# A chunked scan's triangular inverses: two chunks under way at once, one PSUM bank each

## What is computed

```python
def step(state, inp):                      # RWKV-7, one token
    rt, wt, kt, vt, kkt, at = inp
    sa = jnp.einsum('bhij,bhj->bhi', state, -kkt)
    state = (state * wt[:, :, None, :] + sa[..., None] * (kkt * at)[:, :, None, :]
             + vt[..., None] * kt[:, :, None, :])
    return state, jnp.einsum('bhij,bhj->bhi', state, rt)
...
def step(state, inp):                      # HGRN2, one chunk
    scores = jnp.einsum('bhtd,bhsd,bhtsd->bhts', qc, kc, pair)
    out = (jnp.einsum('bhts,bhse->bhte', scores, vc)
           + jnp.einsum('bhtd,bhde->bhte', qc * jnp.exp(cum), state))
```

## Time and profile before

| | us |
|---|---|
| median of 3 runs | 3158.49 |
| lowest and highest run | 3154.6, 3160.9 |
| span of the profiled execution | 3156.2 |

### The profile page before, as it was taken

One profiled execution on the slowest core, in us unless ns is written; L12 is line 12 of the kernel. 1 busy time (PEld: TensorE's weight loads), 2 busy tenths in 40 slices (PEclk: granted clock), 3 DMA queues, 4 the chain that ended last, 5 costly groups with the idle time before them and its releaser, 6 DMA issues. The chain is left out here.

```text
span 3156.2 us, 52466 instructions
## 1 busy us (share of the span) xinstructions
PE 3059.6 (97%) x21178; PEld 2537.2 (80%) x21178; DVE 2152.3 (68%) x3320; ACT 1347.8 (43%) x2189; POOL 498.4 (16%) x650
## 2 busy tenths in 40 slices
PE   8999998899999999999999999999999999999998
PEld 6778776788888788868888888888888887888887
DVE  6777685767765677444445677777877777787786
ACT  6657656555545322023333333333433333444443
POOL 4334343766730011000000000000000000000000
PEclk9999999999999999999999999999999999999999
DMA  6466554212211544311111332333322344777773
GB/s 215 148 197 188 165 182 134 90 63 83 67 36 54 202 153 164 107 54 61 67 66 53 136 112 107 115 118 135 114 107 107 113 143 134 257 216 216 252 224 120
DMA packets 199948, 416.26 MB, mean 132 GB/s; under 512 B 15280, under 2 KB 99504, under 8 KB 193456
## 3 DMA queue, kind: packets, MB, share of 16 engines
q1 hardware_dynamic: 199728, 413.18, 39.6%
HBM read 295.66 MB, written 117.46 MB: 131 GB/s over the span
## 5 line engine op out<-in xcount | busy, mean ns | idle before, releaser
L3068 PE MATMUL ffn_ps<-ffn_t_p,ffn_w_p 128*128 128x512 f32 x2640 | 606.1, 389 | 0.0
L3068 PEld LDWEIGHTS ffn_ps<-ffn_t_p,ffn_w_p 128*128 128x128 f32 x2640 | 495.4, 188 | 103.3 <-DVE ffn_w_p L3243 0.6
L3083 PE MATMUL ffn_ps<-ffn_t_p_parts 128*128 128x512 f32 x1416 | 328.8, 391 | 7.3 <-DVE ffn_t_p_parts L3385 7.3
L3083 PEld LDWEIGHTS ffn_ps<-ffn_t_p_parts 128*128 128x128 f32 x1416 | 267.5, 189 | 63.9 <-DVE ffn_t_p_parts L3385 8.2
L430 POOL TENSOR_TENSOR w_low<-w_ring,w_high 128x1024 fp32r<-128x1024 f32 x84 | 215.6, 2569 | 312.2 <-ACT w_high L584 312.2
L3094 ACT ACTIVATE ffn_w_p<-ffn_w_p_sums 128x512 fp32r<-128x512 f32 x132 | 83.4, 632 | 336.3 <-DVE ffn_w_p_sums L3264 336.1
L546 PE MATMUL proj<-hn_high,w_high 128*128 128x512 f32 x544 | 222.0, 416 | 3.0 <-ACT hn_high L574 1.6
L546 PE MATMUL proj<-hn_high,w_low 128*128 128x512 f32 x544 | 208.6, 392 | 0.0
L546 PE MATMUL proj<-hn_low,w_high 128*128 128x512 f32 x544 | 207.4, 390 | 0.0
L3083 PE MATMUL ffn_ps<-ffn_t_p 128*128 128x512 f32 x696 | 162.5, 389 | 0.0
L3164 ACT ACTIVATE ffn_t_p_parts<-ffn_ring 128x1536 fp32r<-128x1536 f32 x59 | 87.8, 1487 | 158.4 <-PE ffn_ps L3083 147.7
(11 more groups left out here) (547 smaller groups left out, 6745.6 us busy)
## 6 DMA issues: line engine op xcount, KB each, us to landing
ffn_ring<-in_w_up SPq DMA_DIRECT2D x44, 1024.0 KB, 5.4
ffn_ring<-in_w_down SPq DMA_DIRECT2D x88, 512.0 KB, 5.4
w_ring<-in_w_feat SPq DMA_DIRECT2D x84, 512.0 KB, 4.0
ffn_ring<-scratch_values SPq DMA_DIRECT2D x88, 257.0 KB, 4.6
scratch_gates<-ffn_gate SPq DMA_DIRECT2D x44, 512.0 KB, 2.6
ffn_ring<-scratch_gates SPq DMA_DIRECT2D x88, 256.0 KB, 3.9
scan_in<-scratch_scan SPq DMA_DIRECT2D x16, 896.0 KB, 4.4
scratch_values<-ffn_raw SPq DMA_DIRECT2D x22, 513.0 KB, 3.5
```

Source lines behind the costliest of these rows:

```text
L3068: mm = pe.matmul(bank(name, s), w_part(name, a)[:, k * P:(k + 1) * P], t_part(name, b)[:, k * TB:(k + 1) * TB], start=k == a == b == 0, st ...
L3083: mm = pe.matmul(ps[:, DOWN_BANKS[2 * t + c]], down_part(n, x)[:, HID + t * TC:HID + (t + 1) * TC], down_part(n, y)[:, c * DH:(c + 1) * DH ...
```

## The change

- The inverse of a chunk is spread over two passes. In pass i PE computes for chunk m = i + 2 the triangle, the start and levels 0 and 1 (the early part), and for chunk n = i + 1 levels 2, 3, 4 and the corner (the late part). The groups of both chunks and those of chunk i are put into one new order. Each chunk has one bank of `ps_g` for all four heads (bank n % 2), and a level is done at once, not in two halves.
- POOL's masked triangles `off` are gone. `off_times` multiplies with the whole triangle (`low`, negated by ACT as it copies), and DVE lays the mask on afterwards: `w` holds the identity for each level from the start, and `factor` copies only the entries under `lower_mask` out of PSUM, with `copy_predicated`. `start_inverse` is one predicated copy from `low` into `start_inv` in place of a product and a subtraction.
- `lower_mask` is a new table of 128 x 320 fp32, which SP loads at the start of the scan, behind chunk 2, and for which DVE waits before its first step there.
- Preparation is one chunk further ahead (`prepare_mid`, `prepare_kr`, `prepare_d` for i + 3). Features have three buffers, `kr`, `bk` and `small` four, `low` and `invs` two. SP loads chunk i + 4 in pass i.
- The loop starts at i = -3. The S5 pieces stay in their passes and stand elsewhere in DVE's queue.

The diff, cut to its core:

```diff
@@ sync
+            load_chunk(sp, D, I, 2, 2)
+            sp.dma_start(lower_mask[:].rearrange("p m n -> p (m n)"), D["lower"]).then_inc(lower_loaded.sem, 16)
             for name in ("raw", "sign"):
...
@@ gpsimd
-                    for m in range(NI):
-                        pool.tensor_tensor(off[:, m], low[:], heads(level_mask[:, m + 1:m + 2], HD), ALU.mult).then_inc(off_ready.sem, 1)
...
@@ vector
+            dve.tensor_copy(w[:], eye.rearrange("p a (b n) -> p a b n", b=1).broadcast_to([P, NI, H, HD]))
+            start.done(dve.tensor_copy(start_inv[:], eye.broadcast_to([P, H, HD])))
             dve.wait_ge(C["prepared"], 1)
+            dve.wait_ge(*lower_loaded.at(0))
...
             def start_inverse(n):
                 dve.wait_ge(*low_out.at(n))
-                me.done(dve.tensor_tensor(first[:], low[:], heads(level_mask[:, 0:1], HD), ALU.mult))
-                dve.tensor_tensor(invs[:, :, 1], eye.rearrange("p a (b n) -> p a b n", b=1).broadcast_to([P, 2, G2, HD]),
-                                  first[:].rearrange("p (g t) n -> p g t n", g=2), ALU.subtract).then_inc(first_inv.sem, 1)
+                mask = level_mask[:, 0:1].bitcast(I32).broadcast_to([P, H, HD])
+                dve.copy_predicated(start_inv[:], mask, low[n % 2][:]).then_inc(first_inv.sem, 1)
+
+            def factor(n, level):
+                dve.wait_ge(*level_at("y_done", n, level))
+                mask = lower_mask[:, level:level + 1].bitcast(I32).broadcast_to([P, H, HD])
+                dve.copy_predicated(w[:, level], mask, ps_g[:, n % 2, SIDES[0]].rearrange("p (h n) -> p h n", h=H))\
+                   .then_inc(level_sem("w_ready", level), 1)
...
+            def run(i):
+                n, m, p = i + 1, i + 2, i + 3
+                b, late, early, prep = known(i), known(n), known(m), known(p)
+                if late:
+                    factor(n, 2)
+                    first_kind(n)
+                if early:
+                    start_inverse(m)
+                s5_first(i)
+                if late:
+                    prepare_qk(n)
+                if early:
+                    factor(m, 0)
+                if late:
+                    factor(n, 3)
+                    second_kind(n)
+                    picks_first(n)
+                if early:
+                    factor(m, 1)
+                if prep:
+                    prepare_mid(p)
...
+                if b and late:
+                    state_steps(i)
+                if late:
+                    last_kind(n)
+                    factor(n, 4)
+                s5_second(i)
+                if prep:
+                    prepare_kr(p)
...
+                if late:
+                    corner_products(n)
+                    corner_scores(n)
+                    picks_last(n)
@@ tensor
+            def run(i):
+                n, m = i + 1, i + 2
+                b, late, early = known(i), known(n), known(m)
+                if late:
+                    off_times(n, 2)
+                if early:
+                    triangles(m)
+                if late:
+                    new_inverse(n, 2)
+                if early:
+                    first_inverse(m)
+                if b:
+                    right_sides(i)
+                if early:
+                    off_times(m, 0)
+                if late:
                     off_times(n, 3)
+                    first_pairs(n)
+                if early:
+                    new_inverse(m, 0)
+                if late:
+                    second_pairs(n)
+                if b:
+                    solved(i)
+                if late:
                     new_inverse(n, 3)
+                if early:
+                    off_times(m, 1)
+                if b:
+                    grown(i)
+                if late:
+                    third_pairs(n)
                     off_times(n, 4)
+                    third_kind(n)
+                    pairs(n, 2, 1)
+                if b:
+                    outputs(i)
+                if late:
                     new_inverse(n, 4)
+                    pairs(n, 1, 2)
+                    turned(n)
+                if early:
+                    new_inverse(m, 1)
+                if late:
+                    corner_times(n)
+                    last_pairs(n)
+                if early:
+                    first_kind(m)
+                if late:
+                    corner_inverse(n)
+                if early:
+                    second_kind(m)
```

More of the change, by code:

```diff
@@ L1040, in scan_chunks @@
         scores_a = [sb(f"scores_a{u}", [P, H, TC]) for u in range(2)]
-        low = sb("low", [P, H, HD])
+        low = [sb(f"low{u}", [P, H, HD]) for u in range(2)]
         corner_d = [sb(f"corner_d{u}", [P, H, HD]) for u in range(2)]
[L1043 to L1046, removed]
+        start_inv = sb("start_inv", [P, H, HD])
+        invs = [sb(f"invs{u}", [P, 2, H, HD]) for u in range(2)]
+        w = sb("w", [P, NI, H, HD])
+        lower_mask = sb("lower_mask", [P, NI, HD])
         corner_y = sb("corner_y", [P, H, HD])
@@ L1104, in head, with known, level_sem, level_at @@
             return slice((t * 2 + q) * HD, (t * 2 + q + 1) * HD)
-        def heads(mask, n):
-            return mask.broadcast_to([P, H, n])
+        def known(p):
+            return 0 <= p <= LAST
+        def level_sem(name, level):
+            return levels[name][level >= EARLY].sem
+        def level_at(name, p, level):
+            late = level >= EARLY
+            return levels[name][late].at(p, level - EARLY * late)
+        SIDES = (slice(0, H * HD), slice(H * HD, 2 * H * HD))
         def iterations(run):
-            run(-1, -1, 1, 3, False)
-            for i in range(NCH):
-                run(i, i // 2, i % 2, min(3, LAST - i), True)
+            for i in range(-3, NCH):
+                run(i)
         @block.sync
@@ L1453, in _, with run @@
[L1453 to L1461 removed]
+            def run(i):
+                n, m, p = i + 1, i + 2, i + 3
+                b, late, early, prep = known(i), known(n), known(m), known(p)
+                if late:
[16 more added lines that the diff above has]
+                    prepare_mid(p)
+                if i == -3:
+                    for x in (scores_d, state_a, state_d, scores_a, inv):
+                        dve.memset(x[0][:], 0.0)
+                if b and late:
[4 more added lines that the diff above has]
+                s5_second(i)
+                if prep:
+                    prepare_kr(p)
+                if i == -3:
+                    for x in (scores_a, inv):
+                        dve.memset(x[1][:], 0.0)
+                    start.done(dve.memset(diag_a[:], 0.0))
+                if late:
+                    corner_products(n)
+                    corner_scores(n)
+                    picks_last(n)
@@ L1462, in _ @@
+            s5, me = Own(dve, own["s5"]), Own(dve, own["dve_a"])
             iterations(run)
@@ L1506, in off_times @@
[L1506 to L1523 removed]
+                if n >= 2:
+                    hold(inv_out.at(n - 2))
@@ new lines, in first_inverse @@
+                for h in range(H):
+                    for j, r in blocks():
+                        mm = pe.matmul(x_to(n, r, 0, h), start_inv[r, h], ident[r, r], start=True, stop=True)
+                mm.then_inc(x0_done.sem, 1)
+            def off_times(n, level):
+                hold(level_at("x_out", n, level - 1) if level else x0_out.at(n))
+                for h in range(H):
+                    for j, r in blocks():
+                        mm = pe.matmul(x_to(n, r, 0, h), low[n % 2][r, h], invs[n % 2][r, 0, h], start=True, stop=True)
+                mm.then_inc(level_sem("y_done", level), 1)
@@ new lines, in new_inverse, with turned_inv @@
+            def new_inverse(n, level):
+                hold(level_at("w_ready", n, level))
+                def turned_inv(r, h):
+                    return invs[n % 2][r, 1, h] if level else start_inv[r, h]
+                for h in range(H):
+                    for j, r in blocks():
+                        pe.matmul(x_to(n, r, 0, h), turned_inv(r, h), w[r, level, h], start=True, stop=True)
+                    for j, r in blocks():
+                        mm = pe.matmul(x_to(n, r, 1, h), w[r, level, h], turned_inv(r, h), start=True, stop=True)
+                mm.then_inc(level_sem("x_done", level), 1)
```

600 lines of the change are left out of this document (279 added, 321 removed).

## The result

| | before | after |
|---|---|---|
| median, us | 3156.73 | 3135.42 |
| lowest and highest of 4 runs, us | 3154.6, 3160.9 | 3134.29, 3137.55 |
| span of the profiled execution, us | 3156.2 | 3132.5 |

A forecast was written before the change was run, and what follows sets the result against it. PE, busy for 97% of the span, was taken to bound the kernel. Start +12.7, the 14 passes -11.6 and end -4.5 us gave -3.4 us, so 3155.1 us against a median of 3158.49, with a range of 3143.5 to 3167.

The forecast's parts named there:

- (1): PE's instructions and tile-kind changes in a pass: equal in number on both sides, so PE's own work stays 21.3 us.
- (3): New PE waits in a pass, 0.28 us at new_inverse and 0.41 at first_inverse, giving passes of 22.0 us.
- (4): S5 steps moved in DVE's queue: s5_gain no longer stops PE, s5_zeros waits add 1.2; 14 passes 309.2 against 320.8 us.
- (2): PE's old waits in a pass, at corner_times, first_inverse and pairs, go: 0.95 us.
- the walk: Instruction-by-instruction timing from the start of off_times(n, 2): PE free at 0.97, follows DVE's copy at 1.25, new_inverse ends at 2.12 us.
- (5): Start of the scan: DVE's mask wait +6.4 us, filling before the first regular pass +6.3, in all +12.7, bounds 9 and 16.
- the fill: From triangles(0) to the first pass with a finished chunk: 32.5 us against 26.2, +6.3.
- (6): End of the scan: the pass before the last has no early part, 16.5 us against 21.0, -4.5.
- (7): POOL loses five masks a chunk (3.8 us) and DVE one subtraction: neither ends last; deeper loading has room.
- A: Middle gains more: pairs save 0.4 us a pass (-5.6), clock rises during lonely chunk 0 (-3): 3146.5 us, chance 0.30.
- B: start_inverse locked out by POOL, 0.83 us, and factor(n, 2) late: 0.78 us a pass, +10.9, 3166 us, chance 0.17.
- C: In one pass s5_gain still stops PE and the clock falls to 0.5 again: 9.0 us, 3164 us, chance 0.10.

The follow-up runs named there:

- experiment 3: Both kernels with the inverse's ACT and DVE steps, POOL's masks and all waits for them left out: 3124.2 us (before) and 3117.13 us (after).
- Experiment 2: Kernel before, order and halves kept, with predicated copies and no masks on POOL: 3141.74 us with s5_gain, 3138.94 us without.
- Experiment 6: Changed kernel with DVE's wait for lower_mask moved from its first memset of the scan to the first factor: 3131.49 us, ratio 0.9912.
- experiments 1: Kernel before with the s5_gain step left out: 3149.09 us in rounds, ratio 0.9973.
- experiment 5: Kernel before with ACT's second half of the exponentials moved one level later: 3177.78 us in a single run.
- experiment 7: Changed kernel with the late lower_mask wait, second_kind moved behind the next pass's triangles, start_inverse ahead of first_kind on DVE: 3126.44 us, ratio 0.9897.

## Why the prediction was wrong, point by point

- **(1) PE's own work: this step failed.** I put 21.3 us, as 22.27 less the holes that I could see; it is 20.34 at most in the order of before and 20.16 in the order of after. The prediction had named passes under 21.4 us as a sign that it was wrong, and they came. The reason is how a wait looks in a trace of PE. The rows of one single matmul last 0.22 us, but the next may start 0.03 later, so PE can stand still for about 0.2 us with no idle time shown; and where the rows of two groups would have mixed, a wait costs that as well. The pass of after above has such a place: eight instructions of `triangles` from 723.07 are issued by some 723.31, the next group starts at 723.60, 0.36 later than without waits, and the row shows no idle time. The Trainium skill (Perfetto Trace Analysis, Tensor Engine Instruction) says that the end of a TensorE instruction is an estimate of the profiler and no measurement; by that a gap between rows is a lower bound for a wait, and the runs agree: 0.57 us shown, 1.93 lost. I used starts instead of lengths in two places, and trusted the rest to be solid. Even the place that I took as free of waits (581.88 to 582.62, 0.74) had one: without waits it is 0.64. Over 14 passes the step is worth (21.3 - 20.16) x 14 = 16.0 us. With 2.4 from step (3) and 3.9 the other way from step (4), these are the 14.6 us by which the 14 passes fell short of 309.2.
- **(2) Waits that go.** The mechanism held: none of the old waits is left. The size was 1.93 and not 0.95, which is the same error as (1) seen from its other side.
- **(3) Waits that come.** The first is 723.60 where the walk gives 723.62. `start_inv` was taken at 0.62 and is at a median of 0.624:

```profile
L1447 DVE COPY_PREDICATED start_inv<-masks_sb,low x13: 549/624/633, 617.6 to 869.5; 128x256 f32<-128x256 int32 x13
```

  Together they are 0.52 by experiment 3, 0.69 in the forecast; by starts the first is 0.36 and not 0.28, the second 0.17 and not 0.41, though `start_inv` is as long as taken. The pass: 22.0 forecast, 20.68 measured; 1.14 of the difference is step (1), 0.17 this one.
- **(4) S5.** That the stall goes was right: 7.7 to 8.4 us, where I had 9.0. Why it goes, I had only as a possibility, the shorter end of 3.8 to 5.5 us for `s5_gain`. The windows over `s5_gain`'s steps, first of before, then of after, and two of its rows in each:

```profile
644.30:649.80 5.50, 3.07 (x80) 2.67 (x80) 5.19 (x16) 2.61 (x9) 5.40 (x11) 1.00 0.02 4
```

```profile
647.85 0.58 DVE L969 TENSOR_TENSOR s_v<-s_v 128x16 f32<-128x16 f32 x1
648.47 0.65 DVE L970 TENSOR_TENSOR s_v<-s_v 128x16 f32<-128x16 f32 x1
```

```profile
651.00:653.70 2.70, 2.70 (x74) 2.42 (x72) 2.39 (x16) 0.00 (x0) 0.00 (x0) 1.00 0.02 6
```

```profile
653.05 0.17 DVE L970 TENSOR_TENSOR s_v<-s_v 128x16 f32<-128x16 f32 x1
653.25 0.18 DVE L971 TENSOR_TENSOR s_v<-s_v 128x16 f32<-128x16 f32 x1
```

  The same instructions (L969 and L970 became L970 and L971) take 0.17 to 0.18 us with POOL idle and 0.58 to 0.65 with POOL busy for 5.40 of 5.50 us: the fifteen steps take 2.6 us in all instead of 5.5. Without that, DVE would have had `corner_y` about 1.8 us after PE asked for it (an estimate from the rows: 2.9 us more on `s5_gain`'s end at 653.7, `prepare_kr` and the copy behind it, against 656.76). Experiment 2 shows 1.7 of the 2.9 with POOL's masks gone and the order kept. The Trainium skill (SBUF — State Buffer, Who interferes with whom) says that a DVE instruction with two SBUF inputs and a GpSimd instruction that reads SBUF hold a shared port in turn, each for its whole length; these rows agree. I had used that rule for one long copy, where it was worth nothing, and not for fifteen short steps, where it was worth 2.9 us. The 14 passes cost 5.1 us beyond 14 regular ones and not 1.2; the largest is the pass from 661 to 684, 2.4 us, of which 1.39 is PE at rest at 672.29 for no cause that the trace names, and 0.73 a wait for `kc`.
- **(5) Start.** +11.3 against +12.7. DVE's first memset is 6.2 us later than in before (556.72 against 550.48), where I had 7.0, and 1.1 us comes back up to `triangles(0)`, where I had 0.6; the fill is within 0.2. (Its four terms, 3.9, 4.3, 3.9 and 2.3, make 14.4 and not the 14.2 that the sum used.) Experiment 6 shows that the wait for the mask is 3.7 of the 5.2 us; the prediction had put no part of it to DVE's new copies.
- **(6) End.** -4.4 against -4.5.
- **(7) "Neither ends last": this failed too.** DVE's `start_inverse` did end last in the regular passes (0.42 us), and the relief of POOL is part of what shortens `s5_gain`. I had 0.32 of the 0.42 in step (2), but put it down to the second chunk; experiment 2 shows that it needs none.
- **The rivals.** A had the right sign for the wrong reasons. The order gives 0.18 us a pass, not 0.4, and the clock didn't rise early: 0.50 and 0.64 in the windows at the top. B didn't come: `start_inv` never took 0.83 in the 13 passes of the row above. Nor did C. None of them, nor the range, covered an error in PE's own work, since I had taken it for counted, though the text calls it an estimate.

By medians, from 3157.53 us, the median of before beside experiments 1 and 2: 8.4 us are the stall (3149.09), 10.2 the predicated copies and POOL's relief (3138.94), and 3.5 the rest (3135.42), the two chunks under way, the order, and the longer start. In the profiles that rest is 4.7 us at the end of the scan: 14 passes of 293.2 us instead of 307.9 and a last but one of 14.3 instead of 20.5, against 16.5 us more until the first `right_sides` (597.63 instead of 581.17). The intervals of experiment 2 and of after overlap, and against the kernel before of its own rounds each gains 18.6 and 21.3 us, 2.7 apart, so the 3.5 is known in its sign by the traces alone.

## What to carry to other kernels

On an engine that looks busy throughout, don't get its own work by subtracting the idle times that a trace shows: take the distance between starts, compare the same group in places with and without a possible wait, or run the loop once with the waits' causes left out. Before spreading work over two iterations, look at whether the chain itself can be shortened, by fewer instructions or by taking work from the engine beside it: that gave 10.2 us here, and all that came with the second chunk 3.5, since it pays for its passes with a longer start (3.9 of which experiment 6 gives back). And the first wait of a stage should ask only for what the first step reads.

## What the runs showed of the hardware

- Waits of TensorE can cost 0.11 to 0.36 us at a place and leave no idle time in the trace: in before 0.57 us shown and 1.93 lost a pass.
- Two changes of tile kind fewer gave 0.51 us a pass in one order (20.16 to 19.65) and 0.18 in another (1.28 to 1.10 at the two kinds), so the price depends on which groups come to stand together.
- The granted clock fell to 0.50, the level of 1.2 GHz, behind single waits that are shown as 1.03 and 1.12 us, on a PE that was busy before and after, and stayed there for 10 to 14 us; a fall of some 13.5 us cost 5.8 us beside the wait itself (experiment 2), one of 10 us some 3.5 (experiment 5, a pass of 26.6 us instead of 23.1). The length of the wait doesn't decide it: the clock stayed at 1.00 behind five other waits of 1.02 to 1.03 us in the same kernel, behind 1.39 us in after and behind 1.55 us in experiment 7 (618.83). In before, waits shown as 0.23 and 0.34 us in regular passes didn't bring it.
- DVE operations of 16 columns with operands in SBUF take 0.17 us with POOL idle and up to 0.65 beside it; a predicated copy of 256 columns with an SBUF source takes 0.62 beside POOL and 0.45 with POOL idle (experiment 2). With a PSUM source, `factor` had a mean of 0.444 over 80.
